# An encoder trunk on one core: experts' rows added to the output in memory by an indirect accumulating DMA, in place of scatter matmuls and adds into the residual

## What is computed

```python
def moe_swiglu(x, w_router, b_router, w1, w3, w2):
    b, s, d = x.shape
    t = x.reshape(b * s, d)
    logits = jnp.dot(t, w_router, preferred_element_type=jnp.float32) + b_router.astype(jnp.float32)
    top_val, top_idx = lax.top_k(logits, TOP_K)
    top_w = jax.nn.softmax(top_val, axis=-1)
    gates = jnp.sum(jax.nn.one_hot(top_idx, N_EXPERTS, dtype=jnp.float32) * top_w[..., None], axis=1)
    out = jnp.zeros_like(t)
    for e in range(N_EXPERTS):
        he = jax.nn.silu(t @ w1[e]) * (t @ w3[e])
        out = out + gates[:, e:e + 1].astype(t.dtype) * (he @ w2[e])
    return out.reshape(b, s, d)
```

## Time and profile before

| | |
|---|---|
| median of 3 runs | 1437.07 us (1435.19 to 1440.32) |
| the profiled execution's own time | 1439.36 us |
| its span, first to last instruction | 1437.6 us |
| mean granted TensorE clock | 0.976 |
| busy: PE, DVE, ACT, POOL | 1369.8, 1135.7, 933.3, 34.6 us |
| HBM read, written | 413.26 MB, 1.05 MB |

### The profile page before, as it was taken

One profiled execution on the slowest core, in us unless ns is written; L12 is line 12 of the kernel. 1 busy time (PEld: TensorE's weight loads), 2 busy tenths in 40 slices (PEclk: granted clock), 3 DMA queues, 4 the chain that ended last, 5 costly groups with the idle time before them and its releaser, 6 DMA issues.

```text
span 1437.6 us, 17080 instructions
## 1 busy us (share of the span) xinstructions
PE 1369.8 (95%) x7014; PEld 1173.5 (82%) x7015; DVE 1135.7 (79%) x924; ACT 933.3 (65%) x797; POOL 34.6 (2%) x53
## 2 busy tenths in 40 slices
PE   6788999998998999999999999999999999999995
PEld 6677999987977888888888888888888888888884
DVE  5666644447876989988988998898899888899884
ACT  5655433345845777776777777677777777777772
POOL 4200000000000000000000000000000000000000
PEclk9889999999998999999999999999999999999998
DMA  7409656550555999999999999899999989999950
GB/s 237 147 0 334 223 181 199 178 183 23 176 179 219 368 376 372 350 378 335 341 376 368 355 376 377 329 342 373 376 355 375 376 319 349 372 370 366 375 205 32
DMA packets 142421, 415.52 MB, mean 289 GB/s; under 512 B 6899, under 2 KB 39792, under 8 KB 142336
## 3 DMA queue, kind: packets, MB, share of 16 engines
q1 hardware_dynamic: 141760, 414.22, 79.0%
q0 software_dynamic: 576, 0.11, 0.1%
HBM read 413.26 MB, written 1.05 MB: 288 GB/s over the span
## 4 chain that ended last, share of the span: by engine, by line
PE 86%; DVE 8%; ACT 3%; issue 2%; POOL 1%; DMA 0%; SPq 0%; ACTq 0%; DVEq 0%; POOLq 0%
PE ps L561 27%; PE ps L563 27%; PE ps L562 27%; PE ps L917 2%; PE ps L884 1%; DVE w_lo L1374 1%; DVE w_lo L1809 1%; DVE xb_conv L1648 1%; ACT w_hi L1305 1%; PE ps L598 1%; PE ps L896 1%; PE ps L898 1%; DVE expert_in_lo L1789 0%; ACT w_hi L1011 0%; DVE i_then_y L1676 0%
## 5 line engine op out<-in xcount | busy, mean ns | idle before, releaser
L1809 DVE TENSOR_TENSOR w_lo<-w_raw,w_hi 128x2048 fp32r<-128x2048 f32 x333 | 759.9, 2291 | 109.1 <-ACT w_hi L1305 107.0
L1305 ACT ACTIVATE w_hi<-w_raw 128x2048 fp32r<-128x2048 f32 x333 | 638.0, 1919 | 253.4 <-PE ps L563 253.4
L561 PE MATMUL ps<-w_hi,expert_in_hi 128*128 128x512 f32 x896 | 352.0, 393 | 2.8 <-DVE w_lo L1809 2.8
L563 PE MATMUL ps<-w_hi,expert_in_lo 128*128 128x512 f32 x896 | 349.0, 390 | 0.0
L562 PE MATMUL ps<-w_lo,expert_in_hi 128*128 128x512 f32 x896 | 348.8, 389 | 0.0
L561 PEld LDWEIGHTS ps<-w_hi,expert_in_hi 128*128 128x128 f32 x896 | 168.3, 188 | 38.2 <-DVE w_lo L1809 4.5
L563 PEld LDWEIGHTS ps<-w_hi,expert_in_lo 128*128 128x128 f32 x896 | 168.2, 188 | 35.3
L562 PEld LDWEIGHTS ps<-w_lo,expert_in_hi 128*128 128x128 f32 x896 | 168.3, 188 | 33.9
L561 PE MATMUL ps<-w_hi,expert_hT_hi 128*128 128x512 f32 x448 | 174.8, 390 | 0.0
L563 PE MATMUL ps<-w_hi,expert_hT_lo 128*128 128x512 f32 x448 | 174.4, 389 | 0.0
L562 PE MATMUL ps<-w_lo,expert_hT_hi 128*128 128x512 f32 x448 | 174.4, 389 | 0.0
(11 more groups left out here) (313 smaller groups left out, 1203.1 us busy)
## 6 DMA issues: line engine op xcount, KB each, us to landing
w_raw<-in_moe_w_dram SPq DMA_DIRECT2D x336, 1024.0 KB, 5.4
w_raw<-in_ffn_w_dram SPq DMA_DIRECT2D x33, 1024.0 KB, 5.4
w_raw<-in_lru_w_in_dram SPq DMA_DIRECT2D x8, 1024.0 KB, 5.2
w_raw<-in_mla_w_o_dram SPq DMA_DIRECT2D x4, 1024.0 KB, 5.4
w_raw<-in_lru_w_out_dram SPq DMA_DIRECT2D x4, 1024.0 KB, 4.9
w_raw<-in_mla_w_in_dram SPq DMA_DIRECT2D x4, 704.0 KB, 8.0
w_raw<-in_mla_w_qb_dram SPq DMA_DIRECT2D x3, 768.0 KB, 4.4
w_raw<-in_mla_w_kvb_dram SPq DMA_DIRECT2D x2, 1024.0 KB, 9.1
```

Source lines behind the costliest of these rows:

```text
L561: pe.matmul(dst, a[0], b[0], start=start, stop=False)
L563: return pe.matmul(dst, a[1], b[0], start=False, stop=stop)
L1305: act.activation(w_hi[hi_slot(N_PRE + u)][:], raw[slot][:], ACT.Copy).then_inc(hi_ready, 1)
L1809: dve.tensor_tensor(w_lo[s][:], raw[s][:], w_hi[h][:].bitcast(F32), ALU.subtract).then_inc(lo_ready, 1)
```

## The change

The residual is stored to the output before the experts, by GpSimd, and each expert's rows are added to the output in memory: one indirect DMA an expert, issued by GpSimd, takes the 128 slots' rows of `y_out` (128 x 1024 float32) and adds each to the output row whose number stands in `slot_token`. To have that number, the gates get a second column, token number - 512; the product of the selection with both columns gives gate and token - 512 for a used slot, and 0 for an empty one. GpSimd adds 512, so an empty slot has number 512, beyond the bound of 255, and its row is left out. `scatter`, `add_scattered`, `selT`, `y_hi`, `y_lo`, the zero fills and SyncE's stores go. `y_out` is one buffer: ScalarE waits, before it writes it, for the add of the expert before. GpSimd gets its own three checks for overflows, written out.

```diff
-    gates = sbuf.take("gates", [P, TT, E])
+    gates = sbuf.take("gates", [P, TT, E, 2])
...
-            done = experts(sp, body, extra=extra)
-            for i in range(TT):
-                for b in range(2):
-                    at = slice(b * BANK, (b + 1) * BANK)
-                    sp.wait_ge(res_ready, sp.snap(done * 4 + (R_PRE + 2 * i + b + 1)))
-                    sp.dma_start(out[0, i * P:(i + 1) * P, at], res[:, i, at]).then_inc(out_sem, 16)
-            sp.wait_ge(out_sem, 16 * 2 * TT)
+            experts(sp, body, extra=extra)
...
+            own.step(pool.iota(gates[:, :, :, 1], pattern=[[P, TT], [0, E]], base=-NOWHERE, channel_multiplier=1,
+                               allow_small_or_imprecise_dtypes=True))
...
             pool.wait_ge(routed, 1)
-            for b in range(2):
-                pool.memset(y_hi[b][:].bitcast(F32), 0.0).then_inc(y_zeroed, 1)
+            pool.wait_ge(res_ready, R_PRE)
+            for i in range(TT):
+                pool.dma_start(out[0, i * P:(i + 1) * P, :], res[:, i, :]).then_inc(out_sem, 16)
+            pool.wait_ge(out_sem, 16 * TT)
+
+            def add_tokens(n):
+
+                pool.wait_ge(gate_col_ready, n + 1)
+                pool.tensor_scalar(slot_token[:], slot_gate[:, 1:2], float(NOWHERE), None, ALU.add).then_inc(token_ready, 1)
+                pool.wait_ge(token_ready, n + 1)
+                pool.wait_ge(out_ready, 2 * n + 2)
+                pool.indirect_dma_start(out[0], bass.IndirectOffsetOnAxis(ap=slot_token[:, 0:1], axis=0), y_out[:], None,
+                                        bounds_check=SEQ - 1, oob_is_err=False, compute_op=ALU.add).then_inc(added, 16)
+                pool.wait_ge(added, 16 * n + 16)
+
+            for n in range(E):
+                add_tokens(n)
+            pool.wait_ge(keys_sorted, 1)
+            for r in range(OVERFLOWS):
+                key = pool.value_load(top_keys[0:1, r:r + 1], min_val=0, max_val=SEQ * E + E - 1)
+                with pool.If(key > P * E + E - 1):
+                    add_tokens(E + r)
...
-            def scatter(base, number):
-
-                pe.wait_ge(selT_ready, number)
-                for i in range(TT):
-                    for b in range(2):
-                        pe.wait_ge(y_lo_split, base + (b + 1))
-                        pe.matmul(ps[:, 2 + 2 * i + b, :], selT[:, i * P:(i + 1) * P], y_hi[b][:],
-                                  start=True, stop=False)
-                        pe.matmul(ps[:, 2 + 2 * i + b, :], selT[:, i * P:(i + 1) * P], y_lo[b][:],
-                                  start=False, stop=True).then_inc(scattered, 1)
...
-                        pe.wait_ge(selT_ready, n + (d + 2))
...
-                def turn_select():
+                def pick_slots():
                     for i in range(TT):
-                        pe.transpose(ps[:, 7, i * P:(i + 1) * P], sel[:, i, col:col + P].bitcast(F32), ident[:])
-                    for i in range(TT):
-                        ins = pe.matmul(ps[:, 7, SEQ:SEQ + 1], sel[:, i, col:col + P].bitcast(F32),
-                                        gates[:, i, column(e)], start=i == 0, stop=i == TT - 1)
-                    ins.then_inc(selT_turned, 1)
+                        ins = pe.matmul(ps[:, 7, SEQ:SEQ + 2], sel[:, i, col:col + P].bitcast(F32),
+                                        gates[:, i, column(e), :].rearrange("p e c -> p (e c)"), start=i == 0, stop=i == TT - 1)
+                    ins.then_inc(slots_picked, 1)
...
                         if u == M_W1[0, 1]:
-                            if kind != "extra":
-                                scatter(h_base + h0, n + (d + 1))
-                            turn_select()
+                            pick_slots()
...
                 def down(t):
+                    if t == 0 and not (isinstance(n, int) and n + d == 0):
+                        pe.wait_ge(out_ready, h_base + h0)
...
-                    if t == 0 and kind != "extra":
-                        pe.wait_ge(res_ready, s_base + (s0 + 2))
                     up(M_W3, t, 2)
-                    if t == 1 and kind != "extra":
-                        pe.wait_ge(res_ready, s_base + (s0 + 4))
...
-                if kind in ("last", "extra"):
-                    scatter(h_base + (h0 + 2), n + (d + 2))
...
                     if done == M_W1[0, 1]:
-                        act.wait_ge(selT_turned, n + (d + 1))
-                        act.activation(selT[:], ps[:, 7, 0:SEQ], ACT.Copy).then_inc(selT_ready, 1)
-                        act.activation(slot_gate[:], ps[:, 7, SEQ:SEQ + 1], ACT.Copy).then_inc(gate_col_ready, 1)
+                        act.wait_ge(slots_picked, n + (d + 1))
+                        if not (isinstance(n, int) and n + d == 0):
+                            act.wait_ge(token_ready, n + d)
+                            act.wait_ge(out_ready, h_base + h0)
+                        act.activation(slot_gate[:], ps[:, 7, SEQ:SEQ + 2], ACT.Copy).then_inc(gate_col_ready, 1)
...
+                if not (isinstance(n, int) and n + d == 0):
+                    act.wait_ge(added, held(act, 16 * (n + d)))
                 for b in range(2):
-                    act.activation(y_hi[b][:], ps[:, 4 + b, :], ACT.Copy,
-                                   scale=slot_gate[:, 0:1]).then_inc(out_hi_ready, 1)
+                    act.activation(y_out[:, b * BANK:(b + 1) * BANK], ps[:, 4 + b, :], ACT.Copy,
+                                   scale=slot_gate[:, 0:1]).then_inc(out_ready, 1)
...
-            def add_scattered(base):
-
-                for i in range(TT):
-                    for b in range(2):
-                        dve.wait_ge(scattered, base + (2 * i + b + 1))
-                        at = slice(b * BANK, (b + 1) * BANK)
-                        dve.tensor_tensor(res[:, i, at], res[:, i, at], ps[:, 2 + 2 * i + b, :],
-                                          ALU.add).then_inc(res_ready, 1)
...
-                    if done == M_W1[0, 1] and kind != "extra":
-                        dve.wait_ge(res_ready, s_base + (s0 + R_PRE))
-                        add_scattered(s_base + s0)
...
-                for b in range(2):
-                    dve.wait_ge(out_hi_ready, h_base + (h0 + b + 1))
-                    dve.scalar_tensor_tensor(out=y_lo[b][:], in0=ps[:, 4 + b, :], scalar=slot_gate[:, 0:1],
-                                             in1=y_hi[b][:].bitcast(F32), op0=ALU.mult,
-                                             op1=ALU.subtract).then_inc(y_lo_split, 1)
```

More of the change, by code:

```diff
@@ L29 @@
 MISS = 1000.0
+NOWHERE = 512
 TWO_PI_A = 6.28125
@@ L219, in encoder_trunk @@
     top_experts = sbuf.take("top_experts", [P, E], I32)
-    slot_gate = sbuf.take("slot_gate", [P, 1])
+    slot_gate = sbuf.take("slot_gate", [P, 2])
+    slot_token = sbuf.take("slot_token", [P, 1], I32)
     decay = sbuf.take("decay", [P, 2, LRU_HEADS])
@@ L258, in encoder_trunk @@
     m = over(mid.base, 18432)
-    selT = m.take("select_T", [P, SEQ], F32R)
     e_h = m.take("expert_h", [P, CHUNK])
@@ L266, in encoder_trunk @@
     sel = m.take("select", [P, TT, GROUP * P], F32R)
-    y_hi = [m.take("expert_out_hi0", [P, BANK], F32R)]
-    y_lo = [m.take("expert_out_lo0", [P, BANK], F32R)]
     m = over(mid.base + 18432 - 4096, 4096)
-    y_hi.append(m.take("expert_out_hi1", [P, BANK], F32R))
-    y_lo.append(m.take("expert_out_lo1", [P, BANK], F32R))
+    y_out = m.take("expert_out", [P, D])
     far = over(raw_region.base + ATT_SLOTS * UNIT * 4, (RAW_SLOTS - ATT_SLOTS) * UNIT * 4)
@@ L375, in encoder_trunk @@
             sem("ranks_ready"), sem("routed"))
-        sel_ready, gathered, selT_turned = sem("sel_ready"), sem("gathered"), sem("selT_turned")
+        sel_ready, gathered, slots_picked = sem("sel_ready"), sem("gathered"), sem("slots_picked")
         in_hi_ready, in_lo_ready = sem("in_hi_ready"), sem("in_lo_ready")
-        y_lo_split, y_zeroed = sem("y_lo_split"), sem("y_zeroed")
-        selT_ready, gate_col_ready = sem("selT_ready"), sem("gate_col_ready")
+        gate_col_ready, token_ready = sem("gate_col_ready"), sem("token_ready")
         silu_ready, h_ready = sem("silu_ready"), sem("h_ready")
         h_turned, hT_hi_ready, hT_lo_ready = sem("h_turned"), sem("hT_hi_ready"), sem("hT_lo_ready")
-        out_hi_ready = sem("out_hi_ready")
-        scattered = sem("scattered")
+        out_ready, added = sem("out_ready"), sem("added")
         keys_sorted = sem("keys_sorted")
@@ L1349, in first_tokens @@
             def first_tokens():
-                act.activation(selT[:], slot_ids[:], ACT.Copy, scale=0.0).then_inc(selT_ready, 1)
                 take_in(0)
@@ L1765, in _ @@
             own.link(dve.tensor_tensor(second[:], second[:], weight[:, :, 1:2].to_broadcast(shape), ALU.mult))
-            own.step(dve.tensor_tensor(gates[:], first[:], second[:], ALU.add))
+            own.step(dve.tensor_tensor(gates[:, :, :, 0], first[:], second[:], ALU.add))
             dve.wait_ge(ranks_ready, 1)
```

(11 more changed lines are left out.)

8 lines of the change are left out of this document (3 added, 5 removed).

## The result

| | median of its runs | range | profiled execution: time, span |
|---|---|---|---|
| before | 1436.13 us | 1435.19 to 1440.32 | 1439.36, 1437.6 us |
| after | 1421.28 us | 1420.76 to 1421.43 | 1421.23, 1419.5 us |

The ratio is 0.9895, with a 95% interval of 0.9872 to 0.9918: 14.9 us faster. The forecast was 1416.7 us, 20.4 us faster.

What follows compares the result with a forecast made beforehand. TensorE's instructions were taken to bound the expert stage and its sequencer the end. Scatters 14.6, turning 1.8 and end 4.0 sum to 20.4 us off the 1437.07 us median: 1416.7 us, range 1411 to 1426.

Steps and rivals of the forecast that it cites:

- The scatters: Expert stage, TensorE: eight of nine scatters, each 8 matmuls taking 1.82 us between weight units, go; 14.6 us saved.
- turning: Expert stage, TensorE: two transposes of the selection go in each of 8 passes, 0.22 us a pass; 1.8 us saved.
- The tightest place: Start of a pass, unit 2: its converted weights (w_lo) are ready 0.4 us before TensorE wants them, so all is gained.
- The second rival: Pass starts: weight conversion becomes the bound; w_lo 1.0 us late costs 7 us over 7 passes, 1423.7 us; chance 0.08.
- The third rival: Expert stage: GpSimd's adds hold up VectorE's w_lo; 1420.9 us at 1 us delay, 1444.0 at 4.3; chance 0.12.
- the row in the prediction: Profile before: two GpSimd tensor_scalars on 8 elements took 4.62 us beside two VectorE w_lo; GpSimd lost 4.3, VectorE nothing.
- some 24 us in hand: Weight loads in the stage: 30 us from freed slot to use against a 5.4 us landing, so the adds' traffic costs 0.
- So TensorE's end counts: Kernel's end: TensorE's sequencer finishes at 1433.4 us in the old frame, GpSimd at 1428.1 to 1432.5; 4.0 us go.
- GpSimd's drain last: Kernel's end: named sign of a wrong forecast; TensorE's drain was to come last, GpSimd's a little ahead.
- I leave 14.8 as it is: Kernel's end: TensorE's time from entering the overflow checks to its drain, 14.8 us, was kept unchanged after the change.
- The add: Last expert's indirect add on GpSimd: 2.5 to 6.9 us, upper bound from the slowest small GpSimd load; upper bound taken.
- the first rival: Kernel's end: GpSimd ends last if the add takes 7.8 us or more; 1422.7 us at 13.8 us; chance 0.15.

Runs made afterwards that it cites:

- two_adds: The changed kernel with each expert's indirect add issued twice, one after the other; median 1427.17 us, ratio to before 0.9918.
- plain_rows: The changed kernel with the indirect DMAs writing their rows in place of adding them; median 1417.96 us, ratio to before 0.9854.
- after_again: The changed kernel, unchanged, run again for a second profile; median 1420.89 us, ratio to before 0.9890.
- before_again: The kernel before the change, unchanged, run again for a second profile; median 1434.20 us, ratio to before 0.9983.

## Why the prediction came out as it did

**Right, with its mechanism.** TensorE sets the stage's time, and what leaves TensorE leaves the clock. The scatters were put at 1.82 us a pass and measure 1.79; turning was put at 1.8 in all, and 1.46 is left for it; together 15.9 for 16.4. The tightest place, unit 2 with 0.4 us in hand, held: the chain shows no gap at it. The second rival, a conversion that comes late at each start, did not happen: TensorE's waits for w_lo are what they were.

**Right, that GpSimd holds nobody up.** The third rival is out: with 8 or with 16 adds no w_lo is longer than 2.295 us and the stage is unchanged. It is GpSimd that loses. Its tensor_scalar on 128 x 1 elements takes 1.5 to 2.2 us. Each of the eight in after began while a w_lo ran and ended 0.07 to 0.10 us behind it, as in the two timelines above (576.10 + 2.29 against 576.99 + 1.47), so most of its time is waiting. That agrees with the row in the prediction and with "SBUF — State Buffer", section "Who interferes with whom", of the Trainium skill, as far as GpSimd is the later one. Its other half, that VectorE can be the one which waits, no run here shows: no tensor_scalar of GpSimd came first in after, two_adds or plain_rows. The DMA instruction did come first (in the stage of after a w_lo began 0.9 to 1.0 us into each of the seven), and the w_lo kept its 2.29 us.

**Right, that the traffic is hidden.** The adds lengthen the median landing of a weight transfer by 0.5 to 0.9 us at no cost in time (6.3 and 6.2 us in after and after_again, 5.4 and 5.7 in before and before_again). The some 24 us in hand took it up, as forecast.

**The step that failed: "So TensorE's end counts".** The prediction had TensorE's sequencer end the kernel, 14.8 us behind its entry into the checks, and GpSimd at most 10.8 us behind `y_out` (add 6.9, checks 3.9). GpSimd's drain last had been named as a sign of being wrong, and it came; TensorE drained 4.1 us behind its last product, where 13 to 15 had been forecast. The sizes:

- "I leave 14.8 as it is": TensorE needed 7.8 us (1402.3 to 1410.1). The 14.8 are those of an execution with two long branches; with one they are some 6 shorter. A duration that one profile shows once had been taken for a constant; before_again shows the shorter one for the kernel before, too. It also entered the checks 3.5 us ahead of the last matmul's start, not 1.5.
- The add: 6.9 us assumed as upper bound from `y_out` to landing, 7.1 measured (0.8 until the instruction starts, 6.3 for the landing). This was the unknown of the case. That the bound came so near is luck: it was taken from a plain load of 32 KB, and plain rows land in 3.3 us here.
- GpSimd's end behind the landing: 3.9 assumed, 5.0 measured (the checks took 2.4, less than by ScalarE's branches; a drain of 2.4 and 0.2 for the last semaphores were not in the sum at all).

GpSimd therefore ends the kernel 12.1 us behind `y_out`, which is the mechanism of the first rival, though not its cause: the add stayed under the 7.8 us at which that rival was to begin. The tail came to 13.5 us where the forecast's would be 13.2 (17.2 - 4.0): the agreement is a coincidence of two errors, a TensorE end taken too late and a GpSimd end taken too early. Had TensorE's second long branch been there, it would have ended at some 1416 (an estimate, 1410.1 + 6.1), still ahead of GpSimd.

**The median.** The stage and the tail add up to -19.6 us of the profiled span, against -20.4. The forecast then took the whole 20.4 off the median of before, as though each execution had the profiled one's tail. Half of them lie in the lower group, whose one profile has a tail some 6 us shorter. The tail's 4 us are won against the upper group only; against the lower one 1.9 are lost. With the time before at 1434.3 or 1440.0, the change gains 13 or 19 us, and the medians of this comparison lie between, 14.9 apart. The 1.5 us of start in the profiles is scatter from one execution to the next: after_again, the same kernel, starts its first product at 444.88.

## What to carry to other kernels

Where one engine is full from end to end, count the instructions that leave it: that part of the sum held within half a microsecond over 960, and everything beside it really was free. The end is a sum of its own for every engine, down to the drain of the queue, and a step that takes a short chain's place can lengthen it: here the tail with the indirect add is 3.8 us longer than the one with the scatter, adds and stores when both kernels lack the checks, and 1.9 longer when TensorE has one long branch in the kernel before. Before a change is priced against a profile, look whether the times of the kernel before form one group or two, and in which of them the profiled execution lies.

## What the runs showed of the hardware

- A skipped spare pass costs TensorE's sequencer 0.22 us at most of the three branches, and 3.3 to 6.1 us (3.3 to 4.2 at the first, 6.1 at a second) at one or two of them; ScalarE's take 0.05. Of three profiles of the old form with the checks one had two long ones, of nine of the new form none. "Runtime: NRT & Kernel Launch", section "Instruction fetch mechanics", of the Trainium skill says that a taken branch whose target is not in the fetched window has to fetch it by DMA first. The rows agree in so far as nothing but two 16 KB packets of instructions moved during the branch of 6.1 us, and as TensorE, which executed the most instructions by far (7014 matmuls against 924 instructions of VectorE in before), is the one that pays; that the number of stalls varies between executions of one program, with 5.7 us between the groups of times, the page does not say.
- An indirect accumulating DMA with 128 indices, of which 41 to 79 name a row of 4 KB, holds GpSimd 1.6 to 2.3 us for issue (in after) and lands in 5.9 to 6.5 us on idle queues, 9.2 (median) beside the weight stream. Without accumulation it is 1.0 to 1.7 us and 3.3 or 5.8.
- Beside the weight stream the number of rows does not show in the landing: in after the two adds of 41 rows landed in 10.0 and 9.0 us, the two of 79 in 9.3 and 9.2. The landing goes with the place of the expert in its group of two instead: 9.0 to 9.3 us for the first, 10.0 to 10.2 for the second; for plain writes 6.8 to 7.3 and 4.7 to 4.8. Why stays open.
- GpSimd's drain at the program's end takes 82 ns more for each indirect DMA that it has made: 1.79 us after one, 2.36 after eight (accumulating or plain), 3.02 after sixteen.
- GpSimd took 1.5 to 2.2 us in after for a tensor_scalar on 128 single elements that began during a two-input VectorE instruction: it ended 0.07 to 0.10 us behind that one, which itself lost nothing. An indirect DMA's instruction that began ahead of such a VectorE instruction did not lengthen it.
